# One maximum over four banks for both softmaxes of a joint-attention job

## What is computed

```python
def diff_attention(q, k, v, lam, lam_init, subln_g):       # 4 heads, two score sets each
    s = jnp.einsum('bqhid,bkhid->bhiqk', q, k) * (HEAD_DIM ** -0.5)
    p = jax.nn.softmax(s.astype(jnp.float32), axis=-1)
    attn = (p[:, :, 0] - lam * p[:, :, 1]).astype(v.dtype)
    o = jnp.einsum('bhqk,bkhe->bqhe', attn, v)
    ...

def gqa_attention(q, k, v):                                # 8 heads, 2 key/value heads
    ...
    s = jnp.einsum('bqgrd,bkgd->bgrqk', q, k) * (HEAD_DIM ** -0.5)
    p = jax.nn.softmax(s.astype(jnp.float32), axis=-1).astype(v.dtype)
    o = jnp.einsum('bgrqk,bkgd->bqgrd', p, v)
```

## Time and profile before

| | us |
|---|---|
| median of 3 runs | 2779.88 |
| lowest and highest | 2779.04 and 2784.35 |
| the profiled execution | 2779.32 |
| its span | 2777.5 |
| TensorE busy in the span | 2653.7 (96%) |
| VectorE busy | 1595.3 (57%) |
| ScalarE busy | 1050.6 (38%) |
| GpSimd busy | 263.2 (9%) |

### The profile page before, as it was taken

The page is one execution under the profiler, slowest core; times in us unless marked ns, Lnnn a source line. Parts: engine busy times, 40 slices in busy tenths (PEclk is TensorE's granted clock), DMA queues, the critical chain, the costliest instruction groups (busy, mean ns, idle before and its releaser), DMA issues.

```text
span 2777.5 us, 38210 instructions
## 1 busy us (share of the span) xinstructions
PE 2653.7 (96%) x13208; PEld 2191.8 (79%) x13208; DVE 1595.3 (57%) x2506; ACT 1050.6 (38%) x1664; POOL 263.2 (9%) x201
## 2 busy tenths in 40 slices
PE   7999999999999999999989798889999899899997
PEld 6886788887889988888778476678888787788886
DVE  6754655656567756565652684465555655644446
ACT  5234422223347742222341365452233432433333
POOL 2310100001131010000010200120000300300002
PEclk9999999999989999999999899999999999999999
DMA  3221344443310034444412000124444243232222
GB/s 134 69 84 61 121 144 151 143 142 124 120 38 2 1 114 147 140 146 149 159 62 82 8 1 1 44 81 149 145 150 136 78 143 127 76 113 96 93 98 76
DMA packets 77703, 274.36 MB, mean 99 GB/s; under 512 B 8352, under 2 KB 11680, under 8 KB 77088
## 3 DMA queue, kind: packets, MB, share of 16 engines
q1 hardware_dynamic: 58560, 205.55, 22.0%
q10 hardware_dynamic: 19040, 67.43, 7.2%
HBM read 270.84 MB, written 2.10 MB: 98 GB/s over the span
## 4 chain that ended last, share of the span: by engine, by line
PE 82%; DVE 8%; ACT 5%; issue 3%; DMA 1%; POOL 0%; ACTq 0%; DVEq 0%; SPq 0%
PE banks L2217 59%; PE banks L2354 5%; PE banks L2648 3%; PE banks L2260 2%; PE banks L2751 2%; DVE w_lo L1289 2%; PE banks L2736 2%; PE banks L2616 1%; ACT w_hi L656 1%; PE banks L2631 1%; PE banks L2388 1%; PE banks L2716 1%; DMA w_raw<-weights 1%; PE banks L2563 1%; DVE attn_nm L2092 1%
## 5 line engine op out<-in xcount | busy, mean ns | idle before, releaser
L2217 PE MATMUL banks<-h_hi,w_hi 128*128 128x512 f32 x1600 | 627.5, 392 | 3.9 <-DVE w_lo L1289 3.4
L2217 PE MATMUL banks<-h_lo,w_hi 128*128 128x512 f32 x1600 | 624.2, 390 | 0.0
L2217 PE MATMUL banks<-h_hi,w_lo 128*128 128x512 f32 x1600 | 623.9, 390 | 0.0
L656 ACT ACTIVATE w_hi<-w_raw 128x1024 fp32r<-128x1024 f32 x367 | 385.9, 1051 | 550.4 <-PE banks L2217 438.2
L1289 DVE TENSOR_TENSOR w_lo<-w_raw,w_hi 128x1024 fp32r<-128x1024 f32 x367 | 482.6, 1315 | 157.6 <-ACT w_hi L656 139.1
L2217 PE MATMUL banks<-g_hi,w_hi 128*128 128x512 f32 (+1 forms) x1108 | 429.3, 387 | 18.1 <-DVE w_lo L1289 14.6
L2217 PE MATMUL banks<-g_lo,w_hi 128*128 128x512 f32 (+1 forms) x1108 | 423.7, 382 | 0.0
L2217 PE MATMUL banks<-g_hi,w_lo 128*128 128x512 f32 (+1 forms) x1108 | 423.6, 382 | 0.0
L2217 PEld LDWEIGHTS banks<-h_hi,w_hi 128*128 128x128 f32 x1600 | 301.0, 188 | 71.2 <-DVE w_lo L1289 6.8
L2217 PEld LDWEIGHTS banks<-h_hi,w_lo 128*128 128x128 f32 x1600 | 301.2, 188 | 63.0
L2217 PEld LDWEIGHTS banks<-h_lo,w_hi 128*128 128x128 f32 x1600 | 301.2, 188 | 62.1 <-issue 0.7
(11 more groups left out here) (397 smaller groups left out, 3519.2 us busy)
## 6 DMA issues: line engine op xcount, KB each, us to landing
w_raw<-weights SPq DMA_DIRECT2D x384, 512.0 KB, 3.2
ada_raw<-ada ACTq DMA_DIRECT2D x112, 512.0 KB, 3.2
x<-x SPq DMA_DIRECT2D x4, 512.0 KB, 6.8
out<-x SPq DMA_DIRECT2D x8, 256.0 KB, 2.2
mix_cum<-ret_tab ACTq DMA_DIRECT2D x1, 1024.0 KB, 4.8
rows_c<-c_rows ACTq DMA_DIRECT2D x1, 1024.0 KB, 5.0
nsa_w<-cmp_w ACTq DMA_DIRECT2D x1, 1024.0 KB, 7.0
nsa_cbias<-nsa_cbias ACTq DMA_DIRECT2D x1, 1024.0 KB, 9.5
```

The lines of the kernel that those rows point to most:

```text
L656: act.activation(w_hi[s][:], w_raw[s][:], ACT.Copy).then_inc(w_hi_done, 1)
L2217: mm = pe.matmul(bank, w[s][:, k, :], m[:, k, :], start=(n == 0 and a == 0), stop=(n == kts - 1 and a == 2))
```

## The change

One operation takes both maxima of a job. It reads the four banks as two pieces of 768 with a gap between them and writes both numbers a row at once. It waits for the second scores of the job, and with them the first are there too. It adds two to `a_max`, so that both exponentials of the job may start behind it. Nothing else is changed.

```diff
                 if j < ATT_JOBS:
                     if j > 1:
                         dve.wait_ge(a_exp, 2 * j - 2)
-                    for b in range(2):
-                        dve.wait_ge(a_s, 2 * j + b + 1)
-                        sums = banks[:, 2 + 2 * b:4 + 2 * b, :].rearrange("p a t -> p (a t)")[:, 0:NK]
-                        dve.tensor_reduce(B2["nm"][:, j % 2, b:b + 1], sums, AX.X, ALU.max, negate=True)\
-                           .then_inc(a_max, 1)
+                    dve.wait_ge(a_s, 2 * j + 2)
+                    sums = banks[:, 2:6, :].rearrange("p (b a) t -> p b (a t)", b=2)[:, :, 0:NK]
+                    dve.tensor_reduce(B2["nm"][:, j % 2, :], sums, AX.X, ALU.max, negate=True).then_inc(a_max, 2)
                 if j:
                     i = j - 1
                     dve.wait_ge(a_exp, 2 * i + 2)
```

## The result

| | before | after |
|---|---|---|
| median, us | 2780.10 (4 runs) | 2819.61 (4 runs) |
| lowest and highest | 2779.04 and 2784.35 | 2815.08 and 2820.90 |
| profiled execution | 2779.32 | 2818.77 |
| its span | 2777.5 | 2817.0 |

The changed kernel is slower: ratio 1.0136, 95% interval 1.0119 to 1.0154. The forecast was 2815 with a range of 2807 to 2828.

What follows compares the result with a forecast made beforehand. Closed paths through TensorE, one maximum and ScalarE bound both halves. 6.9 (jobs 0 to 4) + 16.8 (5 to 17) + 1.5 (18) + 10.5 (19 to 31) = +35.7 us on 2779.3: 2815.0, range 2807 to 2828.

Steps and rivals of the forecast that it cites:

- One maximum on the path of either half: Both halves: only a job's first maximum is on the path; making it ready later costs 0.81 us.
- The duration: Joint maximum on VectorE: 1.77 us for 2 x 768 elements, with bounds 1.83 and 1.91.
- The differential half turns from a path of two jobs into one of a single job: Jobs 5 to 17: 5.45 us a job instead of 4.16, +16.8 us.
- This wait costs nothing: Grouped half: waiting for the second scores is free, since both score products end together at 1703.00, the maximum starting at 1703.09.
- The signs given for this half: Grouped half, profile after: jobs 7.61 us apart, TensorE's wait for the copy 1.5 us instead of 0.74.
- TensorE's own work of a job: Differential half: about 4.15 us of TensorE work fits into 5.45, leaving it idle some 1.3 us a job.
- Job 18: First exponential starts 3.57 us after the preceding job's second exponential ends, instead of 2.10: +1.5 us.
- The start: Jobs 1 to 4, TensorE's clock partly low: +6.1 us, bounds +3.4 and +8.9; with job 0, +6.9.
- (a): Rival, whole stage: VectorE's instruction count is what counts, so joining helps; 1.6 us saved, 2777.7; chance 3%.
- (b): Rival, first half: TensorE is the bound there and hides the loss, only the second half pays; 2791; chance 7%.
- (c): Rival: TensorE's clock falls with idle time, staying low through jobs 5 to 17; +17.8, 2833; chance 10%.
- the case's own range: The forecast case of 2815, chance 80%: 2812 to 2822 from the start's bounds and a maximum of 1.91.

Runs made afterwards that it cites:

- the late signal alone: Against the kernel before: two maxima, each behind its own scores, but both reported only when the second is done; 2804.5 us, ratio 1.0068 to 1.0096.
- the wait alone: Against the kernel before: still two maxima, but both wait for the job's second scores; 2792.6 us, ratio 1.0029 to 1.0059.
- the copy moved: First turned tile copied ahead of the first exponential, jobs 18 to 31: 2772.1 us against 2780 before; with joint maximum there too 2771.7, in all jobs 2797.8.
- the runs of one half: Against the kernel before: joint maximum only in jobs 0 to 17, 2805.6 us, or only in jobs 18 to 31, 2795.4 us.

## Why the prediction was right, point by point

- *One maximum on the path of either half.* Right. With everything else unchanged, making the first maximum late costs 0.87 us a job in the second half (7.67 against 6.80).
- *The duration*, 1.77 from the slope between two other forms of the maximum: 1.757 measured. The bounds, 1.83 and 1.91, weren't needed. The Trainium skill (VectorE: DVE Perf Modes, section on the perf-mode tiers) has tensor_reduce at 1x only: from 0.957 to 1.757 us, 768 elements more cost 0.800, or 1.04 ns each, and the trace agrees: that is about the rate between 512 and 768 elements, 1.06.
- *The differential half turns from a path of two jobs into one of a single job.* Right, 5.49 us a job for a forecast of 5.45, and 17.7 for 16.8. Of the 0.9 by which it was short, 0.5 is 0.04 us in each of 13 jobs, most of it the start of the maximum behind the scores (0.13 and not 0.09). Another 0.36 is a single job, the first with the grouped keys; see the last section.
- *"This wait costs nothing" in the grouped half.* Wrong by little. The maximum starts 0.18 us after the scores' end in the record and not 0.09, so a job costs 0.89 and not 0.81, 1.0 over 13 jobs. The term that the prediction put at nothing is this wait. With the late signal alone, where the first maximum waits for the first scores only, it starts 0.09 us after the same end of the record (1721.60), and with the wait alone 0.15 us after it (1716.27). So the second scores release VectorE 0.06 us later than the first ones, which the record, with both products beside each other, doesn't show. The other 0.03 us stay open. The signs given for this half come out accordingly: a job of 7.69 and not 7.61, and a wait for the copy of 1.63 and not 1.5.
- *TensorE's own work of a job, about 4.15, and 1.3 us idle.* Too much idle. It is busy for 4.58 us and idle for 0.91. The 4.15 were read from records in which TensorE has no gap; the record of a job's scores includes any wait of the second ones for E, and it grew from 2.24 to 2.44 us. Nothing in the sum hangs on it.
- *Job 18*: its first exponential starts 3.62 us after E for a forecast of 3.57 (1684.97 against 1681.35).
- *The start*: +6.1 expected for jobs 1 to 4 with bounds of 3.4 and 8.9, and +7.4 measured. The term that was short is the share of the clock's lower level, taken as half of the four rounds. The rounds take 6.57, 6.84, 6.42 and 5.99 us, together 3.86 above four times 5.49; of the 4 x 1.37 of the prediction that is 0.70 and not half (an estimate, as all of it is put down to the clock). The windows show the granted clock at 0.50 at 1585 to 1588 and again, after 0.95 at 1594 to 1597, at 1600 to 1603. Before, it was full from 1594 on. The changed kernel first, then the one before:

```profile
1585.00:1588.00 3.00, 1.58 (x3) 0.33 (x2) 1.31 (x1) 0.00 (x0) 0.00 (x0) 0.50 0.00 0
...
1594.00:1597.00 3.00, 1.26 (x6) 0.78 (x5) 2.89 (x5) 1.68 (x4) 0.00 (x0) 0.95 0.00 0
...
1600.00:1603.00 3.00, 3.00 (x16) 3.00 (x15) 2.89 (x5) 1.25 (x3) 0.00 (x0) 0.50 0.00 0
```
```profile
1585.00:1588.00 3.00, 3.00 (x6) 1.59 (x7) 2.39 (x6) 0.99 (x2) 0.00 (x0) 0.50 0.00 0
...
1594.00:1597.00 3.00, 3.00 (x22) 2.59 (x21) 2.89 (x6) 2.43 (x5) 0.00 (x0) 1.00 0.00 0
```

TensorE is busy for 1.58 and 1.26 of 3 us in two of these windows, where it had no gap before. That this idle time is what kept the clock low is argued and not shown.

- *The rivals.* (a), VectorE's instruction count: its busy time fell by 2.7 us and nothing came of it, not even with the copy moved, where the joint operation has room. The Trainium skill (VectorE: DVE Perf Modes, section on the TRN2 errata) prices an operation out of PSUM, the memory of the banks, at 120 cycles beside its elements, 0.125 us in the prediction's estimate. The rows show more: 0.157 of the 0.957 us don't grow with the elements, and here the measurement decides. But two maxima in a row overlap (1.82 us for the pair), so that joining them saves 0.06 us a job, and a saving on an engine that isn't last is no time. (b) fell by the runs of one half. (c), the clock: at 17% idle in one half and 22% in the other it stayed at 1.00; only the start has some of it.

What was short in the sum, 39.5 against 35.7, are these terms: 0.1 for job 0, 1.3 for the start, 0.9 for jobs 5 to 17, 1.0 for jobs 18 to 31 and some tenths outside the stage. All of them err to the same side, so the hit owes nothing to errors that cancel. One step behind the range doesn't follow: 2828 is said to be a third of the way from the case's own range to the clock case, but a third of the way from 2822 to 2833 is 2826.

## What to carry to other kernels

A busy share of 100% does not tell whose path it is. Add up the closed loop from one job to the next with its waits; if the sum hits the rhythm of the trace (8.29 for two jobs here), each link that gets longer costs its whole length as long as no other path is longer, whatever the engines' shares. Joining two operations saves little (0.06 us of 1.82 here), and costs the first reader the second operation's share (0.80 us) and the wait for its input. Do it only where the first result isn't on the loop, and look first at the order in which the reader's engine takes its tasks: moving one copy ahead of one exponential brought 9 us, while the joint maximum brought nothing.

## What was not expected of the hardware

In the three kernels with the joint maximum from job 0 through 17, the maximum of job 16 starts 5.85 us after the one before it, where all others from job 5 on are 5.49 apart:

```profile
1666.26 1.76 DVE L2091 TENSOR_REDUCE attn_nm<-banks 128x2 f32<-128x1536 f32 x1 [1.70 <-PE banks L2749]
...
1672.11 1.76 DVE L2091 TENSOR_REDUCE attn_nm<-banks 128x2 f32<-128x1536 f32 x1 [2.06 <-PE banks L2749]
```

It is the first job with the grouped keys, and the scores' record ends 0.49 us ahead of the maximum instead of 0.13. With the joint maximum from job 5 on, the same job has no such gap (71.39 = 13 x 5.49), nor has it before. The cause stays open; it is worth 0.36 us once.
